# Gathers of two expert slots for 64 tokens, and a weighted sum with folded 64-column diagonals

## The reference

```python
def block(hb):                                   # hb: 128 tokens x 1024
    q = (hb @ w_query).reshape(128, 8, 2, 128)   # 8 retrieval heads
    s = jnp.einsum('nhpd,hpkd->nhpk', q, sub_keys)
    s1, i1 = lax.top_k(s[:, :, 0], 16)
    s2, i2 = lax.top_k(s[:, :, 1], 16)
    cand = s1[..., :, None] + s2[..., None, :]   # 16 x 16 per head
    top, sel = lax.top_k(cand.reshape(128, 8, 256), 16)
    eidx = ...                                   # i1 * 128 + i2 of the chosen
    g = jax.nn.softmax(top, axis=-1)
    act = jax.nn.gelu(jnp.einsum('nd,nhkd->nhk', hb, expert_u[eidx]))
    return jnp.einsum('nhk,nhkd->nd', g * act, expert_v[eidx])
```

## Time and profile before

| | |
|---|---|
| median of three runs | 4192.36 us |
| profiled execution, first to last instruction | 4209.6 us |
| TensorE (PE) busy | 3376.2 us, 80% |
| VectorE (DVE) busy | 2753.6 us, 65% |
| ScalarE (ACT) busy | 1041.5 us, 25% |
| GpSimd (POOL) busy | 1227.4 us, 29% |
| gathers (queue 0) | 1124.27 MB, 67.8% of 16 DMA engines' time |
| mean granted TensorE clock | 0.901 |

### The profile page before, as it was taken

One profiled execution on the slowest core, in us unless ns is written; L12 is line 12 of the kernel. 1 busy time (PEld: TensorE's weight loads), 2 busy tenths in 40 slices (PEclk: granted clock), 3 DMA queues, 4 the chain that ended last, 5 costly groups with the idle time before them and its releaser, 6 DMA issues.

```text
span 4209.6 us, 42927 instructions
## 1 busy us (share of the span) xinstructions
PE 3376.2 (80%) x11308; PEld 1729.8 (41%) x11308; DVE 2753.6 (65%) x7809; ACT 1041.5 (25%) x2385; POOL 1227.4 (29%) x1139
## 2 busy tenths in 40 slices
PE   8799958568887888788888779877887788867877
PEld 2466632243353344334443434343444343522441
DVE  1222211478678769866886788678868876867696
ACT  0233310123323222221232223222322232210221
POOL 0000030024323433433343334323332333334423
PEclk9799879688998998899899989988998899889989
DMA  8111140379998989998999989998999899889988
GB/s 325 53 38 38 39 180 0 115 279 363 368 337 315 413 345 346 367 409 339 339 395 387 360 330 387 381 349 339 395 379 343 324 405 372 317 314 413 384 335 357
DMA packets 299708, 1291.61 MB, mean 307 GB/s; under 512 B 39270, under 2 KB 135414, under 8 KB 163124
## 3 DMA queue, kind: packets, MB, share of 16 engines
q0 software_dynamic: 156672, 1124.27, 67.8%
q1 hardware_dynamic: 142780, 164.51, 12.0%
HBM read 1271.34 MB, written 17.79 MB: 306 GB/s over the span
## 4 chain that ended last, share of the span: by engine, by line
PE 27%; DMA 21%; DVE 17%; issue 12%; ACT 2%; SPq 1%; POOL 1%; DVEq 1%; POOLq 0%; ACTq 0%
PE YY L1571 19%; DMA ring<-experts_dram,idxc 17%; DMA wq<-w_query_dram 4%; PE TT L1560 3%; PE M L1554 3%; DVE ring L1421 2%; DVE dg L1415 2%; DVE yac L1205 2%; SPq L996 1%; POOL ring L1083 1%; DVE eq L1233 1%; DVE eq L1258 1%; DVE eq L1262 1%; DVE bix L1232 1%; DVE bix L1241 1%
## 5 line engine op out<-in xcount | busy, mean ns | idle before, releaser
L1571 PE MATMUL YY<-ring,dg 128*128 128x512 f32 (+1 forms) x4224 | 2095.9, 644 | 549.7 <-DVE dg L1415 547.5
L1083 POOL DMA_INDIRECT ring<-experts_dram,idxc x1056 | 1179.1, 1117 | 2106.2 <-PE YY L1571 1947.0
L1421 DVE CUSTOM_DVE_ANT_0 ring<-ring,h2c 128x1024 f32<-128x1024 f32 x1056 | 1288.4, 1221 | 360.6 <-DMA ring<-experts_dram,idxc 356.8
L1571 PEld LDWEIGHTS YY<-ring,dg 128*128 128x128 f32 (+1 forms) x4224 | 818.4, 202 | 1697.6 <-issue 861.8
L1184 ACT ACTIVATE ga<-act 128x1 f32<-128x1 f32 x1056 | 207.0, 202 | 1521.9 <-DVE act L1421 1520.7
L1415 DVE TENSOR_SCALAR dg<-ident,ga,gc 128x128 f32<-128x128 f32 x1024 | 352.3, 344 | 170.0 <-ACT ga L1184 169.4
L1554 PE MATMUL M<-fT,wq 128*128 128x128 f32 (+1 forms) x2304 | 286.4, 286 | 71.0 <-DMA wq<-w_query_dram 71.0
L1554 PEld LDWEIGHTS M<-fT,wq 128*128 128x128 f32 x2304 | 280.3, 202 | 72.5 <-DMA wq<-w_query_dram 72.5
L1205 DVE SCALAR_TENSOR_TENSOR yac<-win,cw,yac 128x128 f32<-128x128 f32 x960 | 262.4, 344 | 0.0
L530 PE MATMUL A<-w_in,hT 128*128 128x512 f32 (+1 forms) x432 | 213.1, 658 | 0.0
L1184 ACT ACT_TABLE_LOAD x151 | 193.7, 1283 | 2.6
(11 more groups left out here) (291 smaller groups left out, 2578.7 us busy)
## 6 DMA issues: line engine op xcount, KB each, us to landing
wq<-w_query_dram SPq DMA_DIRECT2D x72, 1024.0 KB
wa<-w_ada_dram SPq DMA_DIRECT2D x12, 2048.0 KB, 7.9
ring<-experts_dram,idxc POOLq DMA_INDIRECT x1056
w_in<-w_in_dram SPq DMA_DIRECT2D x1, 10272.0 KB, 33.8
kh<-kT_scratch SPq DMA_DIRECT2D x16, 264.0 KB
xb<-x_prompt_dram SPq DMA_DIRECT2D x8, 512.0 KB, 5.2
t_xb<-x_prompt_dram SPq DMA_DIRECT2D x8, 512.0 KB, 10.7
w_o<-w_o_dram SPq DMA_DIRECT2D x8, 512.0 KB, 5.0
```

The costliest lines, as they stand in the source:

```text
L1083: pool.indirect_dma_start(ring[:, k % RING, :], None, I["experts"], bass.IndirectOffsetOnAxis(idxc[:, k:k + 1], 0)).then_inc(g_in[k % RING ...
L1421: v.tensor_tensor_reduce(out=u, in0=u, in1=h2c[:, :], scale=1.0, scalar=0.0, op0=ALU.mult, op1=ALU.add, accum_out=act8[:, k % RING:k % RIN ...
L1571: mm = pe.matmul(YY[0:w, g * 512:(g + 1) * 512], dg[:, k % DG, 0:w], ring[:, k % RING, D + g * 512:D + (g + 1) * 512], start=(k == 0), sto ...
```

## The change

Gathers of the prompt tiles are laid out anew. Gather k = 2j + g now brings slots 2j and 2j + 1 for the 64 tokens of half g: the first slot on partitions 0 to 63, the second on partitions 64 to 127. The number of gathers and their bytes stay. It follows:

- The expert numbers and the gates are written by four instructions each, of 64 partitions and 8 columns (every second choice), in place of one of 128 partitions and 16 columns. Two of the four read one half of the partitions and write the other.
- h2 is needed twice, once for each half of the tokens, each copied to both halves of the partitions. TensorE makes it with 32 matmuls against the identity in place of 8 transposes; the second copy lies in `SS`. ScalarE writes both straight to `h2c` at the beginning of the next tile (`fold_h2`); the copies `h2n` and L1405 go. The first scores of a tile wait for this.
- The diagonal becomes 128x64: two identities one above the other (`fold2`), scaled by activation and gate.
- TensorE sums two gathers at a time, at every second place, the even gather into rows 0 to 63 of `YY` and the odd one into rows 64 to 127; the order is half of the columns first, then gather.

```diff
+FOLD = 2
+HALF = P // FOLD
-        h2n = sb("h2n", [P, D])
-        h2c = sb("h2c", [P, D])
+        h2c = sb("h2c", [P, FOLD, D])
-        dg = sb("dg", [P, DG, P])
+        dg = sb("dg", [P, DG, HALF])
...
+            def fold_h2(e):
+
+                act.wait_ge(h2_done, e + 1)
+                if some(e):
+                    act.wait_ge(dot_done, NG * e)
+                act.activation(h2c[:, 0, :], TT[:, :], ACT.Copy).then_inc(cur_ready, 1)
+                if not (isinstance(e, int) and e == NB):
+                    act.activation(h2c[:, 1, :], SS[:, :], ACT.Copy).then_inc(cur_ready, 1)
...
-                v.scalar_tensor_tensor(idxn[:, h * TOP:(h + 1) * TOP], ss[:, 0, :], float(NK), ss[:, 1, :],
-                                       ALU.mult, ALU.add).then_inc(idx_ready, 1)
+                    for g in range(FOLD):
+                        i = slice(g * HALF, (g + 1) * HALF)
+                        for s in range(FOLD):
+                            v.scalar_tensor_tensor(idxn[s * HALF:(s + 1) * HALF, h * TOP + g:(h + 1) * TOP:FOLD],
+                                                   ss[i, 0, s::FOLD], float(NK), ss[i, 1, s::FOLD],
+                                                   ALU.mult, ALU.add).then_inc(idx_ready, 1)
...
-                    own.do(v.tensor_scalar(gn[:, h, :] if some(t) else gc[:, h * TOP:(h + 1) * TOP], gn[:, h, :],
-                                           gs[:, 0, h:h + 1], None, ALU.mult))
+                        for g in range(FOLD):
+                            i = slice(g * HALF, (g + 1) * HALF)
+                            for z in range(FOLD):
+                                own.step(v.tensor_scalar(folded[z * HALF:(z + 1) * HALF, h * TOP + g:(h + 1) * TOP:FOLD],
+                                                         ge[i, h, z::FOLD], gs[i, 0, h:h + 1], None, ALU.mult))
+                        own.settle()
...
-                v.tensor_copy(h2c[:, :], h2n[:, :]).then_inc(cur_ready, 1)
-                v.wait_ge(cur_ready, e + 1)
+                    v.wait_ge(cur_ready, FOLD * (e + 1))
...
-                v.tensor_tensor_reduce(out=u, in0=u, in1=h2c[:, :], scale=1.0, scalar=0.0, op0=ALU.mult,
+                v.tensor_tensor_reduce(out=u, in0=u, in1=h2, scale=1.0, scalar=0.0, op0=ALU.mult,
...
+                        for g, bank in ((0, TT), (1, SS)):
+                            for c in range(DC):
+                                for copy in range(FOLD):
+                                    mm = pe.matmul(bank[copy * HALF:(copy + 1) * HALF, c * P:(c + 1) * P],
+                                                   fT[:, c, g * HALF:(g + 1) * HALF], ident[:, :], start=True, stop=True)
...
+                pe.wait_ge(diag_done, NG * e + first + FOLD)
+                for half in range(2):
+                    for k in range(first, first + FOLD):
+                        o = slice(0, w) if smp else slice(k % FOLD * HALF, (k % FOLD + 1) * HALF)
+                        mm = pe.matmul(YY[o, half * 512:(half + 1) * 512], dg[:, k % DG, 0:w],
+                                       ring[:, k % RING, D + half * 512:D + (half + 1) * 512],
+                                       start=(k == 0 if smp else k < FOLD),
+                                       stop=(k == groups_of(e) - 1 if smp else k >= NG - FOLD), skip_group_check=True)
+                        if half:
+                            mm.then_inc(v_done, 1)
...
             def group(e, k):
-                if k:
-                    sums(e, k - 1)
+                if k and k % FOLD == 0:
+                    sums(e, k - FOLD)
```

More of the change, by code:

```diff
@@ L1150, in step @@
                 if s == S_ROUTE + 1:
-                    act.wait_ge(h2_done, t + 1)
-                    if some(t):
-                        act.wait_ge(cur_ready, t)
-                    act.activation(h2n[:, :], TT[:, :], ACT.Copy).then_inc(h2_ready, 1)
+                    if not some(t):
+                        fold_h2(0)
                 if S_ROUTE <= s < S_ROUTE + H:
@@ L1175, in step @@
                     act.wait_ge(sh_ready, H * t + h + 1)
-                    act.activation(gn[:, h, :], top[:, h, :], ACT.Exp, bias=gs[:, 0, h:h + 1],
+                    act.activation(ge[:, h, :], top[:, h, :], ACT.Exp, bias=gs[:, 0, h:h + 1],
                                    accum_out=gs[:, 1, h:h + 1]).then_inc(eg_ready, 1)
@@ L1179, in step, with begin @@
                     assert own.n == OA, own.n
+            def fold_h2(e):
[5 more added lines that the diff above has]
+                    act.activation(h2c[:, 1, :], SS[:, :], ACT.Copy).then_inc(cur_ready, 1)
+            def begin(e):
+                if some(e):
+                    fold_h2(e)
             def gelu(e, k):
@@ L1184, in gelu @@
                 act.activation(ga[:, a:a + 1], act8[:, a:a + 1], ACT.Gelu).then_inc(gelu_done, 1)
-            iterate(act, step, gelu, lambda e: None, lambda e: None, prologue=lambda: act.wait_ge(conv_in, 32))
+            iterate(act, step, gelu, begin, lambda e: None, prologue=lambda: act.wait_ge(conv_in, 32))
         @block.vector
@@ L1368, in step @@
                     own.do(v.reciprocal(gs[:, 0, h:h + 1], gs[:, 1, h:h + 1]))
-                    own.do(v.tensor_scalar(gn[:, h, :] if some(t) else gc[:, h * TOP:(h + 1) * TOP], gn[:, h, :],
-                                           gs[:, 0, h:h + 1], None, ALU.mult))
-                if s == S_ROUTE + 2 and not some(t):
-                    v.wait_ge(h2_ready, 1)
-                    v.tensor_copy(h2c[:, :], h2n[:, :]).then_inc(cur_ready, 1)
-                    v.wait_ge(cur_ready, 1)
+                    if smp:
+                        own.do(v.tensor_scalar(gn[:, h, :], ge[:, h, :], gs[:, 0, h:h + 1], None, ALU.mult))
+                    else:
+                        folded = (gn[:, :, :].rearrange("p h k -> p (h k)") if some(t) else gc)
+                        for g in range(FOLD):
[4 more added lines that the diff above has]
+                        own.settle()
                 if s == S_ROUTE + H + 2 and smp:
-                    v.wait_ge(idx_ready, 8 * t + 8)
+                    v.wait_ge(idx_ready, FOLD * FOLD * (8 * t + 8))
                     v.wait_ge(v_done, NG * (t - 1) + NG // 2)
@@ L1419, in group @@
                 u = ring[:, k % RING, 0:D]
+                if not some(e) and k == 0:
+                    v.wait_ge(cur_ready, FOLD)
+                h2 = h2c[:, 0 if isinstance(e, int) and e == NB else k % FOLD, :]
                 v.wait_ge(g_in[k % RING], 16 * (NG // RING * e + k // RING + 1))
-                v.tensor_tensor_reduce(out=u, in0=u, in1=h2c[:, :], scale=1.0, scalar=0.0, op0=ALU.mult,
+                v.tensor_tensor_reduce(out=u, in0=u, in1=h2, scale=1.0, scalar=0.0, op0=ALU.mult,
                                        op1=ALU.add, accum_out=act8[:, k % RING:k % RING + 1]).then_inc(dot_done, 1)
@@ L1491, in step @@
                         pe.wait_ge(e_done, n)
-                        if h == 0 and some(t):
-                            pe.wait_ge(h2_ready, t)
                         for b in range(nk // P):
@@ L1537, in step @@
                     pe.wait_ge(fT_ready, t + 1)
[L1538 to L1539 removed]
+                    if smp:
+                        for c in range(DC):
+                            mm = pe.transpose(TT[:, c * P:(c + 1) * P], fT[:, c, :], ident[:, :])
+                    else:
+                        for g, bank in ((0, TT), (1, SS)):
+                            for c in range(DC):
+                                for copy in range(FOLD):
+                                    mm = pe.matmul(bank[copy * HALF:(copy + 1) * HALF, c * P:(c + 1) * P],
+                                                   fT[:, c, g * HALF:(g + 1) * HALF], ident[:, :], start=True, stop=True)
                     mm.then_inc(h2_done, 1)
@@ L1562, in project_out, with sums @@
                 return mm
-            def sums(e, k):
-                w = height(e)
-                pe.wait_ge(diag_done, NG * e + k + 1)
-                if k == 0 and some(e):
-                    pe.wait_ge(y_ready, e)
-                for g in range(2):
-                    mm = pe.matmul(YY[0:w, g * 512:(g + 1) * 512], dg[:, k % DG, 0:w],
-                                   ring[:, k % RING, D + g * 512:D + (g + 1) * 512],
-                                   start=(k == 0), stop=(k == groups_of(e) - 1), skip_group_check=True)
-                mm.then_inc(v_done, 1)
+            def sums(e, first):
+                smp = isinstance(e, int) and e == NB
+                w = TS if smp else HALF
+                pe.wait_ge(diag_done, NG * e + first + FOLD)
+                if first == 0 and some(e):
+                    pe.wait_ge(y_ready, e)
+                for half in range(2):
[7 more added lines that the diff above has]
+                            mm.then_inc(v_done, 1)
             def group(e, k):
-                if k:
-                    sums(e, k - 1)
```

(4 more changed lines are left out.)

37 lines of the change are left out of this document (22 added, 15 removed).

## The result

The changed kernel takes 4215.3 us (median of four runs, 4210.95 to 4219.5) against 4194.4 us for the kernel before, timed in turn with it: a ratio of 1.0048, 95% interval 1.0036 to 1.0061. It is slower by half a per cent, by 21 us; 4222 was predicted. Several terms of that sum were far off and cancelled.

What follows compares the result with a forecast made beforehand. A tile was taken as DMA-bound for about two thirds and VectorE-bound for about one third. Terms 50 - 18 - 10 + 8 = +30 us made 4192.4 into 4222 us; range 4205 to 4245, wider 4140 to 4295.

Steps and rivals of the forecast that it cites:

- Its mechanism: Whole tile: VectorE's extra 5 to 8 us outweighs what TensorE gives back; 4205 to 4245 us, chance 0.38.
- VectorE in the routing steps, +50: Routing steps: four number writes and four gate multiplies per head replace one each; 7.1 us per tile, +50 us.
- End of a tile and output projection, -28: Tile's end: h2 copy goes, last pair ends earlier, -18 us; output projection: sums end earlier, -10 us.
- Late slots and the diagonal's wait, +0.7 us a tile: Routing steps and diagonals: slots return late, buffer reuse just fits; 0.7 us a tile, bounds 0 and 3.
- h2 hidden, +0.5 us a tile: Ahead of the first query: h2's longer making hidden by the wait for w_query's third load, except 0.5 us a tile.
- Rival 4: At h2: w_query lands as much later as h2 takes, 6 us in seven tiles; about 4260 us, chance 0.06.
- The reading itself: A tile is DMA-bound for about two thirds, VectorE-bound for about one third; shorter attention steps would show it wrong.
- Rival 3: Sums: the halves don't overlap, 1.2 us of stall in each of six steps, seven tiles; 4297 us, chance 0.11.
- Rival 1: Tile's edge and projection: TensorE's gain prevails, VectorE instructions at 0.085 us or covered; about -38 us, 4154 us, chance 0.25.
- Signs: Sums' busy time 1050 to 1300 us, routing step 17.30 to about 18.5 us, tile's edge 2 us shorter.

Runs made afterwards that it cites:

- single sums: Changed kernel with pairing alone undone, each gather summed by itself right behind its own diagonal into its half of the rows: 4177.7 us, ratio 0.9966.
- the experiment on partitions: Changed kernel with four writes for numbers and for gates, each of 128 partitions and 4 columns, none beginning at another partition: 4183.3 us, ratio 0.9976.
- one write: Changed kernel with a head's expert numbers and its gates each written by one 128x16 instruction again: 4159.4 us, ratio 0.9924.
- the fastest version: Changed kernel with numbers and gates folded once per tile and each gather summed by itself: 4136.3 us, ratio 0.9872.

## Why the predicted total was right and its terms were not

The four pieces that the experiments isolate are: writes +56, pairing +38, overlap -51, h2's making -21. Their sum is +22; measured +21. (They were taken from different versions, h2's with pairs alone, so this agreement is a check and no proof.) The forecast had +50 for the writes, -28 for the two gains by overlap, +5 for late slots and +3.5 for h2. That the total came within 7 us is luck: the last three were off by -23, +33 (the whole of pairing) and -24 us, and these cancel. Its mechanism, VectorE's extra writes outweigh what TensorE gives back, was right in the size of the writes only. With single sums the kernel has the same writes and is faster than before (4177.7 us, 0.9966): it is the cost of the pairs, which the sum put at 5 us, that makes the changed kernel the slower one. Against the prediction's terms:

- *VectorE in the routing steps, +50: right in size, wrong in place.* The prices per instruction held (0.76 and 1.05 us against 0.72 and 1.08), though three of the four are held and not all, as the experiment on partitions shows; the instruction behind them is the fourth that is. Taking the writes away is worth 56 us. But the distance between heads grew by 0.76 us, not 1.2, in tiles 2 to 7 (102.9 to 107.4 over six steps). With one write it is back at 103.0, so half of the 1.46 us is hidden there, and behind what, no run shows. "Tile 0's routing, which few gathers share, I leave out (up to +8 us)" should have stood in the sum: its steps are 5.9 us longer than before (8.8 longer than with one write), and with tile 1's, where the DMA engines were less full before (0.90 against 0.94 from 1714 on), they are most of the visible loss. That the writes are held by their partitions was right for 32 of 56 us; the count costs the rest, 0.07 us for each further write and 0.13 for each further multiply.
- *End of a tile and output projection, -28: the gains exist and were mis-sized.* The overlap as a whole is worth 51 us. VectorE's wait for the projection fell from 78.5 to 50.7 us in all, some 4 us a tile where 1.5 was put (bounds 0 and 3). The tile's edge gave less than its 2.2: from the last dot of a tile to the first of the next it is 1.3 us shorter (14.2 to 12.9, mean of the seven edges between prompt tiles).
- *Late slots and the diagonal's wait, +0.7 us a tile (bounds 0 and 3): the step that failed most.* The mechanism was named rightly (two gathers stay unsummed through the next head's picking) and dismissed by a sum of bytes, "six free slots are enough for five". Measured, held slots cost 18 to 20 us, 2.5 to 3 a tile, and pairing in all 38, some 5 a tile and beyond the bounds. It shows in head 7's numbers to the output, 3.5 us longer, 0.1 shorter than before with single sums. What the other half of pairing's cost is stays open.
- *h2 hidden, +0.5 us a tile: wrong in sign.* x1 to head 0's numbers grew by 4.4 us, and the stretch with the wait behind it is 7.2 us shorter, where h2's time was only to be hidden. Rival 4 expected the load to land later; it lands sooner, and TensorE's waits for w_query fell from 71.0 to 22.8 us.
- *The reading itself held.* In the attention steps the gathers' rate did not move, 425 against 420 GB/s, at a clock of 0.79 against 1.00, and the steps did not get shorter (from a tile's first dot to its fifty-first 137.5 us, 135.9 before, mean of six tiles). The second row is around the slow pair of 1902.77:

```profile
1858.00:1866.00 8.00, 6.30 (x28) 2.56 (x28) 4.81 (x10) 0.61 (x3) 3.68 (x4) 0.79 1.02 425
...
1898.00:1906.00 8.00, 3.23 (x8) 0.77 (x8) 7.41 (x14) 0.81 (x4) 2.69 (x2) 0.64 1.01 412
```

- *Rivals.* Rival 3 is refuted by the 1.94 us of a pair. Rival 1's condition (instructions that go in at 0.085 us each) is nearly met by the run without partition changes, whose numbers and gates cost 0.61 us more per head where the rival had 0.52; it came out at 4183, faster than before, not 4154. The rival that was missing is the fastest version's: that TensorE's gain wins as soon as VectorE and the slots are spared.
- *Signs.* Three of those named for being right did not come: the sums' busy time is 1376 us and not 1050 to 1300, a routing step takes 17.98 us and not 18.5, and the edge of a tile gave less than 2 us.

## What to carry to other kernels

Folding work onto half an array paid here where another engine waited for that array (VectorE for the projection, 81.0 against 50.6 us), and hardly in steps that VectorE fills itself. So look for such waits first, count what the fold costs the engine that is never free, and do it once for many instead of in every step. Don't make one finished item wait for its neighbour when the neighbour stands behind other work in a list, even if the pair is quicker together. When several terms of a sum have opposite signs, test each alone: here four terms of 20 to 60 us made 21.

## What the runs showed that was not expected

- Taking some 3 us of work a tile from TensorE in front of a load (34.6 us of h2 in eight tiles against 9.6) made the kernel 21 us slower (8 to 16 against 17 to 24 us until the load landed).
- 293 us less busy time of TensorE were worth 51 us by overlap; 314 us less again by pairs (1690.1 with single sums to 1376.3) came with a loss of 38.
- At a granted clock of 0.50 a pair takes 3.68 us, as long as two sums without overlap took before at 1.00 (3.60). In the attention steps the granted clock is 1.00 with single sums and 0.79 with pairs.
- The first 800 us, the same in all kernels, took between 808 and 838 us up to the first x1 in the profiled executions; single profiles of this kernel can't be compared by their spans to better than that.
